# Router logits computed the other way round, counts in five products, and three steps of the expert loop reordered

## The reference

```python
def hier_moe(h, w_rg, b_rg, w_re, b_re, w_gate, w_up, w_down):   # h: 512 x 1024
    grp_logits = h @ w_rg + b_rg                    # 4 groups
    grp_sel = argmax(grp_logits); grp_p = softmax(grp_logits)[grp_sel]
    exp_logits = h @ w_re + b_re                    # 32 experts, 8 in a group
    in_logits = exp_logits of the chosen group
    top_p, top_j = top_k(softmax(in_logits), 2)
    gate = grp_p * top_p / sum(top_p)
    expert = grp_sel * 8 + top_j
    # each expert's assigned tokens, in blocks:
    #   (silu(x @ w_gate[e]) * (x @ w_up[e])) @ w_down[e]      (1024 x 512, 1024 x 512, 512 x 1024)
    # each token: sum over its two experts of gate * that row
```

## Time and profile before

| | |
|---|---|
| median of 3 runs | 3553.24 us (3552.72 to 3553.67) |
| profiled execution | 3554.22 us, span 3552.4 us |
| PE busy | 3287.0 us, 93% |
| DVE busy | 2267.4 us, 64% |
| ACT busy | 1466.6 us, 41% |
| POOL busy | 334.0 us, 9% |
| DMA | 522.48 MB, mean 147 GB/s |

### The profile page before, as it was taken

The page is one execution under the profiler, slowest core; times in us unless marked ns, Lnnn a source line. Parts: engine busy times, 40 slices in busy tenths (PEclk is TensorE's granted clock), DMA queues, the critical chain, the costliest instruction groups (busy, mean ns, idle before and its releaser), DMA issues. The chain is left out here.

```text
span 3552.4 us, 46959 instructions
## 1 busy us (share of the span) xinstructions
PE 3287.0 (93%) x18742; PEld 2709.9 (76%) x18742; DVE 2267.4 (64%) x2970; ACT 1466.6 (41%) x1948; POOL 334.0 (9%) x214
## 2 busy tenths in 40 slices
PE   7998989999998998899999998889889999999996
PEld 5887768888887896678787778789667786777774
DVE  6467756656666227668776555656755347888885
ACT  5216723212122116633233343433433136777774
POOL 0020000000000000000000013411100013222221
PEclk8999989999999999999999999999989979999998
DMA  6540013344532221045654239011023249999992
GB/s 240 193 165 13 1 48 107 121 163 130 175 107 87 71 79 43 22 137 190 214 173 127 72 88 273 26 48 58 3 60 89 65 185 360 382 373 366 376 362 93
DMA packets 371657, 522.48 MB, mean 147 GB/s; under 512 B 19618, under 2 KB 313122, under 8 KB 345872
## 3 DMA queue, kind: packets, MB, share of 16 engines
q1 hardware_dynamic: 362112, 503.25, 42.2%
q0 software_dynamic: 9360, 16.72, 1.4%
HBM read 484.46 MB, written 51.90 MB: 151 GB/s over the span
## 5 line engine op out<-in xcount | busy, mean ns | idle before, releaser
L270 DVE TENSOR_TENSOR lo<-exp_raw,exp_hi 128x2048 fp32r<-128x2048 f32 x192 | 438.9, 2290 | 67.7 <-ACT exp_hi L3538 67.7
L3538 ACT CAST exp_hi<-exp_raw 128x2048 fp32r<-128x2048 f32 x192 | 366.3, 1913 | 113.0 <-PE exp_down_acc L265 50.5
L263 PE MATMUL ffn_acc<-normed_hi,up_w_hi 128*128 128x512 f32 (+1 forms) x1056 | 377.3, 357 | 10.3 <-DVE lo L589 6.1
L264 PE MATMUL ffn_acc<-lo,up_w_hi 128*128 128x512 f32 (+1 forms) x1056 | 376.3, 356 | 0.0
L263 PEld LDWEIGHTS ffn_acc<-normed_hi,up_w_hi 128*128 128x128 f32 x1056 | 199.9, 189 | 42.5 <-issue 6.7
L421 DVE SCALAR_TENSOR_TENSOR aside_w<-aside_w,aside_c 128x1024 f32<-128x1024 f32 x176 | 209.5, 1222 | 27.3 <-DMA aside_w<-in_ada_t 20.3
L264 PEld LDWEIGHTS ffn_acc<-lo,up_w_hi 128*128 128x128 f32 x1056 | 200.2, 190 | 31.3
L263 PE MATMUL ffn_acc<-gated_hi,down_w_hi 128*128 128x512 f32 (+1 forms) x528 | 191.6, 363 | 17.6 <-DVE lo L270 17.6
L1238 ACT ACTIVATE conv<-ffn_acc,vecs 128x768 f32<-128x768 f32 (+1 forms) x88 | 73.2, 882 | 288.6 <-PE ffn_acc L265 288.6
L264 PE MATMUL ffn_acc<-lo,down_w_hi 128*128 128x512 f32 (+1 forms) x528 | 190.2, 360 | 0.0
L265 PE MATMUL ffn_acc<-normed_hi,up_w_lo 128*128 128x512 f32 (+1 forms) x528 | 189.0, 358 | 0.0
(11 more groups left out here) (618 smaller groups left out, 8799.2 us busy)
## 6 DMA issues: line engine op xcount, KB each, us to landing
exp_raw<-in_w_experts SPq DMA_DIRECT2D x192, 1024.0 KB, 7.6
aside_w<-in_ada_t SPq DMA_DIRECT2D x176, 512.0 KB, 6.2
up_w<-in_ffn_up SPq DMA_DIRECT2D x88, 512.0 KB, 5.2
x_rows<-dn_zero SPq DMA_DIRECT2D x42, 384.0 KB, 5.3
y_rows<-dn_zero SPq DMA_DIRECT2D x42, 384.0 KB, 5.3
ada_w<-in_ada_first SPq DMA_DIRECT2D x8, 1024.0 KB, 12.3
v<-in_ada_t SPq DMA_DIRECT2D x16, 512.0 KB, 6.2
down_w<-in_ffn_down SPq DMA_DIRECT2D x16, 512.0 KB, 4.3
```

Source lines behind the costliest of these rows:

```text
L263: nc.tensor.matmul(out, left[0], right[0], start=start, stop=False)
L264: nc.tensor.matmul(out, left[0], right[1], start=False, stop=False)
L270: return engine.tensor_tensor(lo, value, hi.bitcast(F32), ALU.subtract)
L3538: nc.scalar.copy(hi[slot(e, j)][:], raw[tile(e, j)][:]).then_inc(tile_hi[j], 1)
```

## The change

**Logits.** For each chunk the router's 128 x 36 is now the weights and `h`'s 128 x 512 the moving side: 8 matmuls into the PSUM tile `lt`, 36 partitions by 512 tokens. VectorE copies it to SBUF (`LT`), and four transposes bring it back to tokens on partitions, in `lp`, which now shares a bank with the block row and no longer lies in `tp`. The transposes of the first row tile stand between the logits and these four, and wait for nothing. `spread` takes one PSUM bank instead of two.

**Counts.** `Ms` has a fifth tile of zeros. One matmul of `before` over all five tiles, and four of `ones` over the first 4, 3, 2 and 1 tiles, each added to the last columns of the result.

**First expert.** TensorE runs `down(0, 0)` ahead of `turn(1, 1)`; ScalarE and VectorE split expert 1's gate tiles ahead of its tokens.

**Last expert.** ScalarE casts the last two down tiles ahead of `finished(NE - 2)`, and VectorE subtracts them ahead of `lo_hidden(NE - 1)`.

```diff
@@ -3104,8 +3104,8 @@
     LATER = TILE_RING - 2
     with ExitStack() as ctx:
         spread_full, scaled, normed = (K.sem("rt_" + n) for n in ("spread", "scaled", "normed"))
-        logits, shifted, exps, shifted2, exps2, assigned, counts, be_ready, bp_ready, dest_ready, turned, rows_out, routed = (
-            K.sem("rt_" + n) for n in ("logits", "shifted", "exps", "shifted2", "exps2", "assigned", "counts", "be", "bp",
+        logits, logits_out, logits_turned, shifted, exps, shifted2, exps2, assigned, counts, be_ready, bp_ready, dest_ready, turned, rows_out, routed = (
+            K.sem("rt_" + n) for n in ("logits", "logits_out", "logits_turned", "shifted", "exps", "shifted2", "exps2", "assigned", "counts", "be", "bp",
                                        "dest", "turned", "rows", "routed"))
         raw_full = [K.sem(f"ex_raw{r}") for r in range(TILE_RING)]
         x_full = [K.sem(f"ex_x{u}") for u in range(2)]
@@ -3123,6 +3123,7 @@
         gain = K.sb(sc, "gain", [P, KD])
         only = K.sb(sc, "first_only", [P, NTX, MB])
         L = K.sb(sc, "logits", [P, NTX, NG + NE])
+        LT = K.sb(sc, "logit_rows", [NG + NE, TX])
         g1, g2, eg, oh = (K.sb(sc, "grp_" + n, [P, NTX, NG]) for n in ("a", "b", "e", "oh"))
         gm, gs = K.sb(sc, "grp_max", [P, NTX]), K.sb(sc, "grp_sum", [P, NTX])
         pick = K.sb(sc, "pick", [P, NTX, EPG, NG])
@@ -3131,7 +3132,7 @@
         top = K.sb(sc, "top", [P, TOPK, NTX])
         m0, m1 = K.sb(sc, "max_a", [P, NTX]), K.sb(sc, "max_b", [P, NTX])
         M = K.sb(sc, "assigned", [P, TOPK, NTX, NE])
-        Ms = K.sb(sc, "assigned_any", [P, NTX, NE])
+        Ms = K.sb(sc, "assigned_any", [P, NTX + 1, NE])
         cnt, nb, ca, cb, start = (K.sb(sc, "cnt_" + n, [P, NE]) for n in ("n", "blocks", "a", "b", "start"))
         where = K.sb(sc, "where", [P, NTX, NE])
         beyond = K.sb(sc, "beyond", [P, NTX, NE])
@@ -3148,11 +3149,13 @@
             flat = K.x.rearrange("p c t -> p (c t)")
             y, xr = ([flat[0:MB, (2 * n + u) * D:(2 * n + u + 1) * D] for u in range(2)] for n in range(2))
         with ExitStack() as pc:
-            spread = K.ps(pc, "spread", [P, 2, TX])[:, 0, :]
+            spread = K.ps(pc, "spread", [P, TX])[:]
+            lt = K.ps(pc, "route_logits", [P, TX])[0:NG + NE, :]
             cp = K.ps(pc, "route_counts", [P, NTX + 1, NE])
-            bp = K.ps(pc, "route_blocks", [P, P])
+            blocks_bank = K.ps(pc, "route_blocks", [P, 512])
+            bp = blocks_bank[:, 0:P]
+            lp = blocks_bank[:, P:P + NTX * (NG + NE)].rearrange("p (t n) -> p t n", t=NTX)
             tp = K.ps(pc, "route_turned", [P, 2, D])
-            lp = tp[:].rearrange("p u (s n) -> p (u s) n", s=2)[:, :, 0:NG + NE]
         with ExitStack() as pc:
             xt = K.ps(pc, "exp_turned", [P, KD, P])
             gp = K.ps(pc, "exp_gate_acc", [P, DE])
@@ -3267,23 +3270,27 @@
             last.then_inc(spread_full, 1)
             for c in range(KD):
                 pe.wait_ge(normed, c + 1)
-                for t in range(NTX):
-                    last = nc.tensor.matmul(lp[:, t, :], h[:, c, t * P:(t + 1) * P], wr[:, c, :], start=(c == 0), stop=(c == KD - 1))
+                last = nc.tensor.matmul(lt, wr[:, c, :], h[:, c, :], start=(c == 0), stop=(c == KD - 1))
             last.then_inc(logits, 1)
-            pe.wait_ge(shifted, 1)
-            for t in range(NTX):
+
+            def rows_of(t):
                 if t >= 2:
                     pe.wait_ge(rows_out, t - 1)
                 for c in range(KD):
                     last = nc.tensor.transpose(tp[:, t % 2, c * P:(c + 1) * P], h[:, c, t * P:(t + 1) * P], ident)
                 last.then_inc(turned, 1)
+
+            rows_of(0)
+            pe.wait_ge(logits_out, 1)
+            for t in range(NTX):
+                last = nc.tensor.transpose(lp[:, t, :], LT[:, t * P:(t + 1) * P], ident[0:NG + NE, 0:NG + NE])
+            last.then_inc(logits_turned, 1)
+            for t in range(1, NTX):
+                rows_of(t)
             pe.wait_ge(assigned, 1)
-            for t in range(NTX):
-                for b in range(t):
-                    nc.tensor.matmul(cp[:, t, :], ones, Ms[:, b, :], start=(b == 0), stop=False)
-                nc.tensor.matmul(cp[:, t, :], before, Ms[:, t, :], start=(t == 0), stop=True)
-            for t in range(NTX):
-                last = nc.tensor.matmul(cp[:, NTX, :], ones, Ms[:, t, :], start=(t == 0), stop=(t == NTX - 1))
+            nc.tensor.matmul(cp[:], before, Ms[:], start=True, stop=False)
+            for b in range(NTX, 0, -1):
+                last = nc.tensor.matmul(cp[:, NTX + 1 - b:NTX + 1, :], ones, Ms[:, 0:b, :], start=False, stop=(b == 1))
             last.then_inc(counts, 1)
             for t in range(NTX):
                 pe.wait_ge(rows_out, NTX + t - 1)
@@ -3328,11 +3335,14 @@
             rank_e = K.const("expert_rank").unsqueeze(1).broadcast_to([P, NTX, EPG])
             nc.vector.scalar_tensor_tensor(gain[:], K.mod[:, 0, scale_at:scale_at + KD], 1.0, K.vec(weight_at), ALU.add, ALU.mult)
             dve.drain()
+            nc.vector.memset(Ms[:, NTX, :], 0.0)
             dve.wait_ge(spread_full, 1)
             for c in range(KD):
                 nc.vector.scalar_tensor_tensor(h[:, c, :], K.x[:, c, 0:TX], gain[:, c:c + 1], spread, ALU.mult,
                                                ALU.mult).then_inc(scaled, 1)
             dve.wait_ge(logits, 1)
+            nc.vector.tensor_copy(LT[:], lt).then_inc(logits_out, 1)
+            dve.wait_ge(logits_turned, 1)
             tt(L[:], lp, K.row("b_router").unsqueeze(1).broadcast_to([P, NTX, NG + NE]), ALU.add)
             dve.drain()
             rd(gm[:], L[:, :, 0:NG], AX_X, ALU.max)
@@ -3388,7 +3398,7 @@
                        oh[:, t, :].unsqueeze(2).broadcast_to([P, NG, EPG]),
                        chosen[:, k, t, :].unsqueeze(1).broadcast_to([P, NG, EPG]), ALU.mult)
             dve.drain()
-            tt(Ms[:], M[:, 0], M[:, 1], ALU.add).then_inc(assigned, 1)
+            tt(Ms[:, 0:NTX], M[:, 0], M[:, 1], ALU.add).then_inc(assigned, 1)
             tt(m0[:], top[:, 0, :], top[:, 1, :], ALU.add)
             dve.drain()
             nc.vector.reciprocal(m0[:], m0[:])
@@ -3501,8 +3511,8 @@
             gate(0, 0)
             lift(0, 0)
             turn_hidden(0)
+            down(0, 0)
             turn(1, 1)
-            down(0, 0)
             for e in range(1, NE):
                 gate(e, e)
                 if e + 1 < NE:
@@ -3577,8 +3587,10 @@
             for j in DOWN:
                 hi_tile(0, j)
             hi_hidden(0)
+            for j in GATE:
+                hi_tile(1, j)
             hi_tokens(1, 1)
-            for j in GATE + UP:
+            for j in UP:
                 hi_tile(1, j)
             for e in range(1, NE):
                 if e >= 2:
@@ -3589,10 +3601,11 @@
                     hi_tokens(e + 1, (e + 1) % 2)
                     for j in GATE + UP:
                         hi_tile(e + 1, j)
+                else:
+                    for j in DOWN:
+                        hi_tile(e, j)
                 finished(e - 1)
                 hi_hidden(e)
-            for j in DOWN:
-                hi_tile(NE - 1, j)
             finished(NE - 1)
             n = n_over(act)
             with act.Fori(0, NOVER // 2) as jt:
@@ -3641,8 +3654,10 @@
             hidden(0, turn_of[0, UP[1]] + 1)
             lo_tile(0, 0, DOWN[1])
             lo_hidden(0)
+            for j in GATE:
+                lo_tile(1, 1, j)
             lo_tokens(1, 1)
-            for j in GATE + UP:
+            for j in UP:
                 lo_tile(1, 1, j)
             for e in range(1, NE):
                 if e >= 2:
@@ -3655,9 +3670,10 @@
                 if e + 1 < NE:
                     for j in (1, 2, 3):
                         lo_tile(e + 1, e + 1, j)
+                else:
+                    for j in DOWN:
+                        lo_tile(e, e, j)
                 lo_hidden(e)
-            for j in DOWN:
-                lo_tile(NE - 1, NE - 1, j)
             n = n_over(dve)
             with dve.Fori(0, NOVER // 2) as jt:
                 for u in range(2):
```

## The result

Changed: 3530.87 us, median of five (3526.93 to 3531.65). Before: 3552.72, median of five; the two runs added to the three shown above came out lower (3545.18, 3547.11). The profiled execution took 3529.11 us, its span is 3527.3, 25.1 shorter than before's.

A forecast was written before the change was run, and what follows sets the result against it. The prediction held that TensorE's pace, not the weight transfers, bounds the expert loop. Routing 5.2, first expert 3.9 and last expert 4.6 us sum to 13.7, off 3553.24: 3539.5 us, range 3535.5 to 3545.5 with rivals A and B.

The forecast's parts named there:

- Part 1a: Routing logits: 16 halves instead of 64, the first 5.9 us at half clock, 9.8 us together, saving 4.1 us.
- Rival A: Routing: the new logits stay at half clock and take 13.3 us; total gain 9.9 us, 3543.3 us; chance 0.11.
- D: Logits and most of down(0) at half clock, no clock gain at the last expert; 3546.7 us; chance 0.06.
- Part 1b: Routing, turning the logits back: the bias addition comes 2.0 us later behind them; bounds 1.2 to 3.4.
- Part 1c: Routing counts: five products take 2.3 us instead of 5.5, saving 3.1 us; bounds -0.4 to 4.2.
- Part 2: First expert: down(0) ahead of turn(1) starts gate(1) 3.9 us sooner; at best 4.7, at worst -2.0.
- Part 3: Last expert: earlier down-tile casts save 3.6 us of waiting plus 1.0 by the clock, 4.6 us; bounds 3.6 to 5.4.
- Rivals B and C: B: expert 1's tokens come late, 3543.4 us, chance 0.07; C: weights bound the loop from expert 2, 3556.5 us, chance 0.03.
- R: Ahead of the routing, posed with the experiments: the change itself makes unchanged earlier stages 9 us faster; no chance given.

The follow-up runs named there:

- e11: Changed kernel with the order of the first expert put back, so routing and last expert as changed; 3536.33 us, ratio 0.9956.
- e1: The kernel before, unedited, run again against itself; 3545.73 us, ratio 0.9988.
- e4: Kernel before plus only the last expert's two down tiles split sooner, and the longer table Ms; 3546.45 us, ratio 0.9994.
- e5: Kernel before plus only the first expert's new order and earlier gate-tile splits, and the longer table Ms; 3547.66 us, ratio 0.9995.
- e7: Kernel before with only the 14 count products replaced by the new five, old logits kept; 3546.47 us, ratio 0.9989.
- e6: Kernel before with only the new logits, counts still in 14 products; 3545.92 us, ratio 0.9980.
- e9: The kernel before, unedited, run a third time against itself; 3548.81 us, ratio 0.9998.
- e8: Changed kernel plus idle fp32 products of constants where TensorE stands still; 3527.69 us, ratio 0.9932 to the kernel before.
- e3: Changed kernel with first and last expert put back, so only logits and counts as changed; 3538.02 us, ratio 0.9969 to before.
- e12: The pause-filled changed kernel plus three more idle products in the routing and expert 1's tokens turned inside down(0); 3525.30 us, ratio 0.9928 to before.

## Why the prediction was wrong

The direction held, and so did the work and the waits that each part was to take away; the size and the range didn't.

**"A saving worked out in the span is taken off 3553.24"** failed. The forecast set its sum against one profiled execution and three timed runs within 1 us of each other, and took them for the kernel's time. Later runs of the same kernel lay between 3541.01 and 3557.67, the medians of its sets of runs between 3545.7 and 3552.7, and in the profiles the same code reached the logits at times 9 us apart. A range of 10 us left no room for that, though the forecast itself calls 7.1 us what a measurement can tell from no change. In numbers: all 94 timed runs of the kernel before average 3549.8 us, the 15 of the changed kernel 3530.3, which is 9.2 under the forecast. Of these, 3.4 are the base, which was high for this kernel; 2.5 are the terms (16.2 in place of 13.7); and 3.3, with a standard error of 0.8, lie in none of its steps.

By parts, between the means of three profiles, the terms are 7.8 for the routing (5.2 forecast), 3.3 for the first expert (3.9) and 5.1 for the last one (4.6). The term that was most mis-sized is the routing: its counts, and the chain behind them, were priced at half clock or left as they were, and ran at full.

**Part 1a, the logits** (9.8 us forecast, 9.91 measured) held, clock course and all: half until 2873.4, full behind. Rival A fell, and D with it: in every profile with the new logits the clock rose while they ran, or stood full.

**Part 1b, the way back** (2.0 forecast) measured 1.43: from 2877.52 to 2878.95. It was priced with the 1.5 us of half-clock transposes; at full clock the eight took 1.09.

**Part 1c, the counts** (2.3 us forecast, 1.39 measured) was mis-sized. The price per half was right in kind: ten halves, the widest pair a little dearer. But the prices came from rows at half clock, and the counts ran at full. The bounds had allowed for that (saving up to 4.2, measured 4.1); the value taken hadn't. (The sum writes 3.1 for 5.5 less 2.3, which is 3.2.) The rest of TensorE's chain, which the forecast moved without shortening it, took 7.51 us from the copy to the gathering, where the earlier trace rows have 8.52: the transposes of x took 0.20 us each there (6.50 for 32) and at full clock 0.12 (1.94 for 16). The forecast had put this at nothing without a reason. In sum routing 7.6 against 5.2 in the two profiles shown: 0.6 for the way back, 0.9 for the counts, 1.0 for the chain behind, less 0.1 for the logits.

**Part 2, the first expert** (3.9 forecast). From the end of the hidden transposes to gate(1) it is now 2930.51 - 2918.56 = 11.95 us, in the earlier trace rows 15.01: 3.1. The waits were right (2.06 and 1.88); down(0) took its half-clock stretch in full, 7.19 us to the turn where 6.35 were taken, which is the 0.8. B shows 4.7 because in before one more stretch lay in gate(0), row below, where the changed kernel has full clock (2906 to 2918). But a fall in gate(1), which the forecast didn't have, takes 1.6 back in C. Before:
```profile
2924.00:2927.20 3.20, 3.20 (x9) 2.17 (x8) 3.20 (x2) 2.29 (x2) 2.90 (x2) 0.50 0.66 255
```
**Part 3, the last expert** (4.6 forecast). The wait went from 5.36 to 1.73, 3.6 as said. The 1.0 us taken for a clock that stays up didn't come: it was at half for 3.4 us in the last down products. And where it did stay up, in e11, E was no shorter (50.4). That the term still came out near, 5.1, is luck: E is 1.5 us shorter between the means of three, of which the run of half clock in down(31), 4.1 us before (to 3504.1) and 3.4 after, gives some 0.3. The rest is of the size by which E differs between profiles of kernels with the same last expert (50.3 to 52.4 as before, 48.9 to 50.7 as changed).

**Rivals B and C** fell: no wait for tokens, and in the loop TensorE waits once, 0.9 us for a hidden, as in the earlier trace rows.

**What stays open.** Whether the change makes the time ahead of it shorter, by less than R had said. Each kernel's timed gain (one less the ratio, times the median of before) can be set against its gain in the changed part. In the eight kernels with the new logits the timed gain is larger every time, by 1.2 to 5.6 us, 3.8 on average; in the five with the old ones it is from 3.8 larger to 3.8 smaller, on average 0.7 smaller. Each has an interval of some 4 us to either side. Taken the other way, the timed runs less the changed part of the kernel's profiles leave a time ahead of the logits: on average 2869.7 us for the eight sets of runs with the new logits (2867.4 to 2871.7), 2873.3 for the nine with the old ones, of which only e1's (2869.7) is not above all eight. In the profiles the logits start at 2869.8 on average with the new ones, at 2872.2 with the old ones, spread over 14 and 9 us. So R is refuted at 9 us, but some 3.5 us point to it, if the changed part takes as long in the timed runs as in the profiles, which they can't show. e4, e5 and e7 have the longer table and no such gain, so it isn't that one; e6 has the gain with the old counts, so it goes with the new logits and what they brought (`LT`, `lt`, `lp`, the smaller spread). None of these was tried alone, and no mechanism for it was seen.

## What to carry to other kernels

Before a sum of small terms is set against a time, run the unchanged kernel several times over and compare it with itself, and compare the time to the first changed instruction in both traces: what differs there is not the work of the change's steps. Give short fp32 work a price for either clock, and ask for each step which the change will meet, since shortening one step moves where the clock falls in the next. A pause of TensorE of some two microseconds can have a second price, behind it.

## What the hardware showed beside

- One kernel reached the same instruction 9.0 us apart in two executions (2876.7, 2867.7), with 198.6 and 188.9 us at half clock before it. Half of the difference, 4.9 us, is the most that those 9.7 us at half can cost; in a third (e9) it was 2872.2 with 185.4 us. So the clock accounts for a part of it only.
- In the changed kernel the clock fell behind pauses of 1.73 to 2.06 us, in all three profiles. The falls lasted 3.4 us and cost 1.5 to 1.6 us where the loop went on behind them; products of constants in the pauses took them away (e8). But one pause had a fall behind it in some kernels and none in others: the 1.93 us ahead of gate(0) in before and e11 and not in the changed kernel, e3, e8 and e12; the 1.88 us ahead of gate(1) in the changed kernel and not in e5; the 1.74 us ahead of the last down products in the changed kernel and not in e11.
- Work alone did not raise it soon: 20.75 us busy of 23.50 in e7, all at 0.50, as in the earlier trace rows. The Trainium skill ("TensorE: Matmul & The Clock Gate", "What's actually happening") has activity release the gate, which e8 and e12 bear out and this row of e7 doesn't.
- The gather of expert 1's tokens, issued at 2914.65 in e12, let its turn start at 2925.22: 10.6 us, under a DMA share of 1.02. In the changed kernel it was issued at 2916.60, and the turn at 2927.80, 11.2 us later, did not wait for it. Row and stretch of e12:
```profile
2914.65 2.80 POOL L3239 DMA_INDIRECT x<-x_rows,filled  x1 [1.95 <-DMA x_rows<-h_rows,dest]
...
2914.60:2925.20 10.60, 6.58 (x26) 3.71 (x27) 6.94 (x4) 4.09 (x3) 5.57 (x2) 1.00 1.02 359
```
